# Two of the mixer's six gate projections as one group of seven half-size products, dealt over the levels of gated linear attention

## The reference, cut to what matters

```python
proj = h @ w_in                      # h: 256 x 1024; the last 3072 columns are gate_logits
...
gates = jax.nn.sigmoid(gate_logits + b_gate).reshape(B, S, N_BRANCHES, D_MODEL)
y = gates[..., 0, :] * o_mla + gates[..., 1, :] * o_gla + gates[..., 2, :] * o_mem
x = x + y @ w_o
```

## Time and profile before

| | before |
|---|---|
| runs (3) | 970.54, 970.54, 969.59 us; median 970.54 us |
| profiled execution | 969.14 us, its span 967.2 us |
| PE / DVE / ACT / POOL busy | 954.4 / 697.0 / 220.4 / 23.2 us |
| granted TensorE clock | 1.000 |
| the loop of nine iterations | from 220.4 to 300.4 us of the span |

### The profile page before, as it was taken

How to read it: one execution, slowest core, us unless ns; L and a number is a source line. 1 busy time by engine, 2 the same in 40 slices (tenths; PEclk the granted TensorE clock), 3 DMA queues, 4 the chain that set the end, 5 groups by cost and what they waited for, 6 DMA issues and landing times.

```text
span 967.2 us, 12513 instructions
## 1 busy us (share of the span) xinstructions
PE 954.4 (99%) x5014; PEld 590.6 (61%) x5014; DVE 697.0 (72%) x1259; ACT 220.4 (23%) x438; POOL 23.2 (2%) x27
## 2 busy tenths in 40 slices
PE   7999999999999999999999999999999999999998
PEld 6944445754555449999844469458854444468544
DVE  4866964586566887866899763888965969674667
ACT  4313422223241232422200011001011321434200
POOL 0000000000002500000000000000000000000000
PEclk9999999999999999999999999999999999999999
DMA  9551731443345624344454443425243434321631
GB/s 329 149 196 43 283 130 44 174 134 128 97 158 155 182 109 169 115 175 175 174 174 173 174 149 124 164 88 175 87 138 124 173 116 150 109 105 45 218 130 44
DMA packets 53818, 139.76 MB, mean 144 GB/s; under 512 B 3968, under 2 KB 7904, under 8 KB 53760
## 3 DMA queue, kind: packets, MB, share of 16 engines
q1 hardware_dynamic: 52304, 135.07, 39.7%
q0 software_dynamic: 1248, 3.80, 1.7%
q10 hardware_dynamic: 208, 0.08, 0.0%
HBM read 137.90 MB, written 1.05 MB: 144 GB/s over the span
## 4 chain that ended last, share of the span: by engine, by line
PE 92%; DVE 5%; ACT 1%; issue 1%; DMA 0%; DVEq 0%; ACTq 0%
PE pair L1947 36%; PE pair L2032 18%; PE pair L2028 16%; PE pair L2286 6%; PE turned L1892 4%; PE score L2286 3%; DVE arena L928 3%; PE turned L2286 1%; PE score L2381 1%; PE score L2457 1%; PE score L2131 1%; PE score L2444 1%; PE score L2183 1%; PE score L2130 1%; PE score L2199 1%
## 5 line engine op out<-in xcount | busy, mean ns | idle before, releaser
L1947 PE MATMUL pair<-ring,hT 128*128 128x512 f32 (+2 forms) x640 | 269.8, 576 | 0.9 <-ACT hT L600 0.9
L928 DVE TENSOR_TENSOR arena<-arena 128x512 f32<-128x512 f32 (+6 forms) x329 | 194.1, 604 | 13.4 <-PE score L2286 4.1
L1947 PEld LDWEIGHTS pair<-ring,hT 128*128 128x128 f32 x640 | 119.2, 190 | 130.5 <-issue 125.5
L1947 PE MATMUL pair<-hT,ring 128*128 128x128 f32 (+2 forms) x464 | 76.4, 324 | 0.2 <-ACT hT L600 0.2
L928 DVE TENSOR_TENSOR arena<-pair,arena 128x512 f32<-128x512 f32 x57 | 39.4, 691 | 46.6 <-PE pair L2032 22.7
L2032 PE MATMUL pair<-ring,arena 128*128 128x512 f32 x160 | 71.7, 594 | 0.0
L1947 PEld LDWEIGHTS pair<-hT,ring 128*128 128x128 f32 (+1 forms) x464 | 66.0, 188 | 9.0 <-issue 1.3
L928 DVE TENSOR_TENSOR arena<-ring 128x2048 f32<-128x2048 f32 (+1 forms) x37 | 67.7, 1831 | 2.5 <-DMA ring<-in_w_ssm_out 1.3
L2032 PE MATMUL pair<-arena 128*128 128x512 f32 x144 | 65.3, 595 | 0.3 <-DVE arena L928 0.3
L2028 PE MATMUL pair<-arena 128*128 128x128 f32 x544 | 64.0, 276 | 0.0
L2032 PE MATMUL pair<-ring,hT 128*128 128x512 f32 x136 | 62.4, 598 | 0.8 <-DMA ring<-in_w_in 0.8
(11 more groups left out here) (221 smaller groups left out, 1004.4 us busy)
## 6 DMA issues: line engine op xcount, KB each, us to landing
ring<-in_w_in SPq DMA_DIRECT2D x33, 2048.0 KB, 8.4
ring<-in_w_up SPq DMA_DIRECT2D x8, 2048.0 KB, 8.5
ring<-in_w_down SPq DMA_DIRECT2D x8, 2048.0 KB, 7.8
ring<-in_w_o SPq DMA_DIRECT2D x4, 2048.0 KB, 7.9
ring<-in_w_mem_kv SPq DMA_DIRECT2D x2, 2048.0 KB, 7.8
ring<-in_w_glu SPq DMA_DIRECT2D x2, 2048.0 KB, 7.8
ring<-in_w_ssm_out SPq DMA_DIRECT2D x2, 2048.0 KB, 7.8
ring<-in_w_ukv SPq DMA_DIRECT2D x4, 512.0 KB, 3.7
```

The source lines that it names most:

```text
L928: return dve.tensor_tensor(o, a, b, op)
L1947: ins = pe.matmul(o_, s, m, start=a, stop=b)
```

## The change

Gates 0 and 1 (1024 columns) become one group, GT, between MV and the feed-forward's groups. Its rows are summed at h=8, its seven products are dealt over iterations 0 to 3, its sums and blocks over VectorE's iterations 0 to 3. Bias 0 is added as block 11 leaves PSUM; bias 1 is added to the temporary v, from which blocks 12 and 22 are made; v less bias 0 serves block 21. One sigmoid over all 2048 elements and one multiplication replace two of each. gate4 and gate5 are now filled at i=4 to 6 (two quarters each) and i=7, 8 (one quarter each).

```diff
-RG, MV, UP = 3, 4, 5
+RG, MV, GT, UP = 3, 4, 5, 6
...
-    j = [(f"gate{i}", "w_in", C_GATE + 512 * i, 512) for i in (0, 1, 4, 5, 2, 3)]
+    out += halves(GT, C_GATE)
+    j = [(f"gate{i}", "w_in", C_GATE + 512 * i, 512) for i in (4, 5, 2, 3)]
...
-ORDERS[UP] = ORDERS[WP] = (1, 2, 5, 7, 3, 6, 4)
+ORDERS[GT] = ORDERS[UP] = ORDERS[WP] = (1, 2, 5, 7, 3, 6, 4)
...
-        sum_t2 = [r_gla, r_gla, r_gla, arena[:, dec_at:dec_at + 2048], arena[:, dec_at:dec_at + 2048]]
+        sum_t2 = [r_gla, r_gla, r_gla, arena[:, dec_at:dec_at + 2048], arena[:, dec_at:dec_at + 2048], memT]
...
+            if i == GT:
+                return mq_tok, mk_tok, mk_tok, mq_tok
```

GpSimd:

```diff
             for n, i in enumerate(GATES):
-                if n >= 2:
+                if n in (2, 3):
+                    pool.wait_ge(sem("last_out"), GT + 1)
+                elif n >= 4:
                     pool.wait_ge(sem("taken_dve"), taken(f"gate{GATES[n - 2]}")[1])
```

ScalarE:

```diff
             for i in range(9):
                 if i < 8:
                     level_exp(i)
+                if i == 1:
+                    group_copy(GT, 5)
                 if 1 <= i <= EH:
                     turned(softT[:, 512 * ((i - 1) % 2):512 * ((i - 1) % 2) + 512], 512)
                 if i < EH:
                     exps("mem", i, ((0, 256, 0), (256, 256, 1)))
-                if i in (4, 6, 8):
-                    gate_sigmoid((i - 4) // 2)
+                if i == 0:
+                    group_copy(GT, 1)
+                if i == 4:
+                    act.wait_ge(sem("first_out"), GT + 1)
+                    act.wait_ge(sem("second_out"), GT + 1)
+                    act.wait_ge(sem("last_out"), GT + 1)
+                    act.activation(gate_buf, gate_buf, ACT.Sigmoid).then_inc(sem("gate_sig"), 1)
+                if i == 8:
+                    gate_sigmoid(2)
```

VectorE (the last hunk stands at the end of an iteration, behind the levels' work):

```diff
+                if i == GT:
+                    dve.wait_ge(sem("group_product"), product_at(MV, 4))
...
                 if h == 8:
                     group_t3(MV)
                     m_squares(0)
+                    group_rows(GT)
...
             for i in range(9):
+                if i == 0:
+                    group_t1(GT)
                 if i == 1:
                     group_last(MV, vm4[2])
+                    group_t3(GT)
+                    dve.wait_ge(sem("bgate0"), 16)
+                    dve.wait_ge(sem("group_product"), product_at(GT, 2))
+                    link(tt(gt4[0], h[1], bgate[:, 0:512], ALU.add))
...
-                if i in (3, 5, 7):
-                    gate_take((i - 3) // 2)
-                if i in (5, 7):
-                    gate_apply((i - 5) // 2, (i - 5) // 2 + 1)
+                if i == 1:
+                    group_t2(GT)
+                if i == 2:
+                    group_t4(GT)
+                    group_z(GT)
+                if i == 3:
+                    group_v(GT)
+                    dve.wait_ge(sem("bgate1"), 16)
+                    link(tt(biased, v, bgate[:, 512:1024], ALU.add))
+                    dve.wait_ge(sem("group_product"), product_at(GT, 3))
+                    mark(tt(gt4[1], h[3], biased, ALU.add), "first_out")
+                    mark(tt(gt4[3], z, biased, ALU.add), "second_out")
+                    link(tt(v, v, bgate[:, 0:512], ALU.subtract))
+                    group_last(GT, gt4[2])
+                if i == 5:
+                    dve.wait_ge(sem("gate_sig"), 1)
+                    link(tt(o_mla, o_mla, gate_buf, ALU.mult))
+                if i == 7:
+                    gate_take(2)
```

TensorE:

```diff
             for i in range(9):
-                if i:
-                    fill(["gate0", "gate1", "gate4", "gate5"], i - 1, 2)
+                if i < 4:
+                    for g, q in (((MV, 4), (GT, 1)), ((GT, 2), (GT, 5)), ((GT, 7), (GT, 3)), ((GT, 6), (GT, 4)))[i]:
+                        group_multiply(g, q)
+                elif i < 7:
+                    fill(["gate4", "gate5"], i - 4, 2)
                 else:
-                    group_multiply(MV, 4)
+                    fill(["gate4", "gate5"], i - 1, 1)
```

More of the change, by code:

```diff
@@ L126 @@
 ORDERS = {i: (1, 5, 2, 7, 3, 6, 4) for i in range(NG)}
-ORDERS[UP] = ORDERS[WP] = (1, 2, 5, 7, 3, 6, 4)
+ORDERS[GT] = ORDERS[UP] = ORDERS[WP] = (1, 2, 5, 7, 3, 6, 4)
 ORDERS[RA] = (1, 5, 2, 7, 6, 3, 4)
-ROWS = (0, 1, 1, 2, 3) + 4 * (4,) + (5, 5, 6, 7, 8)
+ROWS = (0, 1, 1, 2, 3, 4) + 4 * (5,) + (6, 6, 7, 8, 9)
 LAST_JOB = {job[1]: job[0] for job in JOBS}
@@ L147 @@
         HALVES += [(_n, _t) for _t in range(2) for _n in _pair]
-BY_DVE = {"gg", "wo0", "wo1", "ao0", "ao1"} | {f"gate{i}" for i in range(6)}
+BY_DVE = {"gg", "wo0", "wo1", "ao0", "ao1"} | {f"gate{i}" for i in range(2, 6)}
 SPLIT_TOKENS = ("us0", "us1")
@@ L230, in act_at @@
 def act_at(i, n):
-    return 3 * i + n - max(i - SO, 0)
+    return 3 * i + n - max(i - SO, 0) - (i > GT)
 def product_at(i, q):
@@ L325, in build @@
         copied_q1, copied_q5, sum_z, sum_v = a1(512), junk[:, 0:512], across, junk[:, 512:1024]
-        sum_t2 = [r_gla, r_gla, r_gla, arena[:, dec_at:dec_at + 2048], arena[:, dec_at:dec_at + 2048]]
+        sum_t2 = [r_gla, r_gla, r_gla, arena[:, dec_at:dec_at + 2048], arena[:, dec_at:dec_at + 2048], memT]
         sum_t3 = arena[:, r_at + 2048:r_at + 4096]
-        sum_rows = [knT, mem_tok, mem_tok, arena[:, dec_at + 2048:dec_at + 4096], arena[:, dec_at + 2048:dec_at + 4096]]
+        sum_rows = [knT, mem_tok, mem_tok, arena[:, dec_at + 2048:dec_at + 4096], arena[:, dec_at + 2048:dec_at + 4096], qnT]
         a2 = Place()
@@ L413, in group @@
                 t2, t3 = (x.rearrange("p (k n) -> p k n", n=512) for x in ((sum_t2[i], sum_t3) if i < UP else (up_t2, up_t3)))
-                if i in (RG, MV):
+                if i in (RG, MV, GT):
                     t3 = b12
@@ L625, in square_first @@
                 group_first(i, quarter_of_hidden(i, 0))
-                act.wait_ge(sem("group_act"), 3 * i + 3)
+                act.wait_ge(sem("group_act"), act_at(i, 3))
                 act.activation(quarter_of_hidden(i, 0), quarter_of_hidden(i, 0), ACT.Square).then_inc(sem("ff_ready"), 1)
@@ L985, in group_t1 @@
                 weights_in(f"g{i}x")
-                if i and i != RA:
+                if i == GT:
+                    dve.wait_ge(sem("group_product"), product_at(MV, 4))
+                elif i and i != RA:
                     dve.wait_ge(sem("group_product"), product_at(i - 1 if i != GLU else RS, 6))
@@ L1337, in _ @@
             level_diff(0)
+            gt4 = by_tokens(gate_buf)
+            h, (_, _, z, v), biased = group(GT)[0], temporaries(GT), ckv[:, 0:512]
             for i in range(9):
+                if i == 0:
+                    group_t1(GT)
                 if i == 1:
                     group_last(MV, vm4[2])
+                    group_t3(GT)
+                    dve.wait_ge(sem("bgate0"), 16)
+                    dve.wait_ge(sem("group_product"), product_at(GT, 2))
+                    link(tt(gt4[0], h[1], bgate[:, 0:512], ALU.add))
                 if i < EH:
@@ L1406, in _ @@
             mark(tt(o_gla, o_gla, r_gla, ALU.mult), "mixer_out")
-            gate_apply(2, 3)
-            gate_apply(3, 4)
+            gate_apply(2, 2)
+            gate_apply(3, 3)
             link(tt(o_mla, o_mla, o_mem, ALU.add))
@@ L1417, in _ @@
                     g = gate_buf[:, 1024 * (n % 2) + 512 * t:1024 * (n % 2) + 512 * t + 512]
-                    dve.wait_ge(sem("gate_sig"), 4 + 2 * t + n - 3)
+                    dve.wait_ge(sem("gate_sig"), 3 + 2 * t + n - 3)
                     link(tt(og3[:, t, c:c + 512], og3[:, t, c:c + 512], g, ALU.mult))
```

## The result

The changed kernel took 988.69 us (median of four runs, 987.98 to 990.16) against 970.07 for the kernel before (now four runs): a ratio of 1.0196, 95% interval 1.0183 to 1.0209, 18.6 us slower.

What follows compares the result with a forecast made beforehand. The prediction took TensorE, busy 954.4 of 967.2 us, as the bound. Waits of 16.7 us less 3.4 gained gave 13.3 slower, 983.8 from 970.54; one clock fall of 1.7 made 985.5, range 982.0 to 991.0.

Steps and rivals of the forecast that it cites:

- The clock: In the loop, one fall of TensorE's granted clock behind the longest wait, costing 1.7 us; chance 0.34.
- The gain: TensorE's gate products: the group has 28 products for 32, one product of a group saved, 3.44 us.
- Wait 1: Before the loop, GT's product 1 waits for MV's `first_out`, delayed by the row sums; 1.6 us lost.
- Wait 2: Behind level 0, GT's product 2 waits for ScalarE's copy of product 1, behind head 0's exponentials; 3.3 us lost.
- Wait 3: At i=3, GT's product 4 waits for T4 and z from the end of VectorE's iteration 2; 5.0 us lost.
- Wait 4: At i=4, gate4 waits for GT's `first_out`, three operations behind the end of VectorE's iteration 3; 6.5 us.
- The last: At i=8, the copy of level 8 comes later than the second value product wants it; 0.3 us, an estimate.
- second rival: Clock falls behind both long waits, each costing 1.7 us: 987.2, up to 991.3; chance 0.22.
- upper bound: Clock's worst case: all TensorE work between wait 3 and wait 4 at half speed, 7.5 us more.
- The first rival: The waits in TensorE's list without any fall of the clock: 983.8 us; chance 0.30.
- The third: VectorE ahead of TensorE at the ends of iterations 2 and 3, long waits vanish: down to 967.1; chance 0.04.
- The fourth: One long wait is shorter, VectorE having caught up more than counted: 975 to 981 us; chance 0.10.

Runs made afterwards that it cites:

- take_at_6: all_early with gate4's bias addition moved from the end of VectorE's iteration 7 to the start of 6; 966.52 us, 0.9966 of the kernel before.
- all_early: The changed kernel with GT's row sums, T4, z, blocks and ScalarE's copy of product 1 all placed earlier, same work; 967.02 us.
- rows_at_7: The changed kernel with only GT's four row sums moved from h=8 to h=7; 985.96 us.
- the pauses: Four kernels, each the kernel before plus one early TensorE wait of 2.64 to 5.81 us and no work; 973.63 to 978.98 us.
- copy_early: rows_at_7 with ScalarE's copy of GT's product 1 also moved ahead of the exponentials of head 0; 983.73 us.

## Why the prediction was right, point by point

The direction, the mechanism and the range (982.0 to 991.0) held; 985.5 was 3.2 us too low. As a slowdown it was 15.0 us for 18.6 measured, 3.6 short, since the median of the kernel before came to 970.07 and not 970.54. The clock's term was 3.7 short. The order of the working:

- **The gain.** Set at 3.44 us for one product. take_at_6, where nothing in the loop waits, shows 3.41 in the rows and 3.1 between medians; all_early, with the last wait of 0.44, shows 2.9 between medians.
- **Wait 1.** Set at 1.6, ahead of GT's product 1, for MV's `first_out`. It was 1.93, ahead of MV's product 4, for ScalarE's copies. The cause (row sums at h=8 push all of VectorE's list) was right, and rows_at_7 shows it; the place was wrong. I had looked for VectorE's results that TensorE asks for, and not for those of ScalarE that hang on VectorE's: sigmoid, silu, sigmoid, copy. It came first and covered the one that I had counted. That the wrong place cost the sum so little has a reason. The release of product 2 does not hang on wait 1: the chain that ended last runs through VectorE's list to the maxima, then through ScalarE's exponentials and copy to product 2. Waits 1 and 2 together are how late that copy comes, 1.6 + 3.3 = 4.9 as set and 1.93 + 2.81 = 4.74 as measured; what TensorE loses at the first it doesn't lose at the second.

```profile
232.03 0.42 DVE arena L1222
232.50 0.18 DVE stats L1227
232.73 0.39 issue
233.12 0.68 ACT arena L713 x3
233.79 0.49 ACT arena L618
234.28 0.14 issue
234.42 8.80 PE pair L2072 x16
```

- **Wait 2.** 3.3 set, 2.81 measured: TensorE got there 0.6 later than I had it (231.2, less the 0.4 of the start), 0.3 of that by the larger wait 1. The releaser was ScalarE's copy (L618), behind the exponentials, as said.
- **Wait 3.** 5.0 set, 4.99 measured. **Wait 4.** 6.5 set, 6.62 measured. **The last.** 0.3 set, 0.44 measured.
- **The sum of the waits** was 16.7 and is 16.8; that it is so near is partly luck, since waits 1 and 2 together were set 0.2 too long, wait 4 and the last 0.3 too short. The local reckoning held: from where level i left TensorE to the end of VectorE's iteration i, taken from the trace of before, plus the new operations.
- **The clock** is the term that was mis-sized. I took one fall at 1.7 us, behind the longest wait; there were three, 5.4 us, one of them behind wait 2, of 2.8 us, for which the prediction counts no fall. My second rival, both long waits paid (0.22, from 987.2), was nearer than the forecast. The price of one, 1.7 from the kernel's first matmuls, is near the 1.6 to 2.1 of the change and the lower end of what the pauses cost by themselves (1.7 to 3.1). The upper bound counted only the work between waits 3 and 4 at half speed; products behind waits 2 and 4 slowed as well, so it was no bound; the three falls together cost 5.4 us, under its 7.5. The Trainium skill (TensorE: Matmul & The Clock Gate, "HAM oscillation") warns of pauses in mid-kernel, and these runs bear it out with granted clocks of 0.72 and 0.76 behind them.
- **The first rival** (waits alone, 983.8) falls with the granted clock: 0.993 over the whole kernel. **The third**, VectorE ahead of TensorE, was false for the change as written and is what all_early makes true. **The fourth**, one long wait shorter than counted, is out: they were 4.99 and 6.62.
- **Behind the loop** nothing drifted: 19.8 us at `y`, 19.8 at the next chain.

## What to carry to other kernels

Where one engine is busy all the time and a helper has idle time, ask at which point of the helper's list the idle time lies. It lay ahead of the scores of each iteration, and the change put its sums behind them: with the same 15 us of added work the change lost 18.6 us, and won 3.1 from the product saved once that work stood on the other side of the wait. Before moving work into a list with slack, take from the trace, for each result, when it is asked for and what stands between, through every engine of the chain; and count a pause of TensorE at full clock as its length plus, in this kernel, 0 to 3.1 us more.

## What the runs showed of the hardware

The granted clock can fall behind a pause of TensorE as short as 2.3 us (rows_at_7: eight instructions in 5.37 us behind it, for 3.60, and a granted clock of 0.72 from 232 to 238 us), and stayed up behind one of 2.90 in two executions of four. The same pause of 4.98 to 4.99 us cost 1.6 us of slow products in the change and 3.0 in copy_early. The clock was back within the sixteen instructions of 128x512 that followed a pause of 6.62 us: they took 9.23 us, and the next sixteen 7.13.
